# Where ScalarE's function tables are loaded in the first block's attention stage

## What is computed

```python
z = h @ w_in
q, k, v = heads(z[..., :ATT_W]), heads(...), heads(...)
att = _neighbourhood_attention(q, k, v, kc, vc, rpb, rows)   # softmax over a window and a context

def _spatial_gating(u, v, ln_g, ln_b, w_s, b_s):
    u = jax.nn.gelu(u)
    v = _layernorm(jax.nn.gelu(v), ln_g, ln_b)
    ...
    return u * mixed

def _conformer_conv(a, gate, w, b, ng, nb):
    h = a * jax.nn.sigmoid(gate)
    ...
    return jax.nn.silu(h)
```

## Time and profile before

| | us |
|---|---|
| median of 3 runs | 1346.89 |
| lowest and highest | 1346.85, 1347.02 |
| the profiled execution | 1347.08 |
| its span, first to last instruction | 1345.8 |
| PE busy in the span | 1328.6 |
| ACT busy in the span | 628.7 |
| DVE busy in the span | 826.0 |

### The profile page before, as it was taken

One profiled execution on the slowest core, in us unless ns is written; L12 is line 12 of the kernel. 1 busy time (PEld: TensorE's weight loads), 2 busy tenths in 40 slices (PEclk: granted clock), 3 DMA queues, 4 the chain that ended last, 5 costly groups with the idle time before them and its releaser, 6 DMA issues.

```text
span 1345.8 us, 17461 instructions
## 1 busy us (share of the span) xinstructions
PE 1328.6 (99%) x6892; PEld 1105.1 (82%) x6892; DVE 826.0 (61%) x1171; ACT 628.7 (47%) x911; POOL 54.7 (4%) x73
## 2 busy tenths in 40 slices
PE   9999999999999999999999999999999999999998
PEld 6787877888888888889887787788898888888886
DVE  5679876685554443335535544444877865667897
ACT  6646768453333333223434455333734333434764
POOL 0000000000001111111000000000000500000000
PEclk9999999999999999999999999999999999999999
DMA  9734412323367677776232111223604625323764
GB/s 378 309 123 149 147 54 81 135 95 141 141 189 192 175 191 180 200 184 168 85 111 77 63 64 71 71 94 111 202 17 164 266 94 141 110 95 117 223 208 133
DMA packets 55152, 193.46 MB, mean 144 GB/s; under 512 B 6368, under 2 KB 8672, under 8 KB 53664
## 3 DMA queue, kind: packets, MB, share of 16 engines
q1 hardware_dynamic: 46448, 156.04, 34.1%
q0 software_dynamic: 8624, 36.31, 10.9%
HBM read 184.46 MB, written 28.05 MB: 158 GB/s over the span
## 4 chain that ended last, share of the span: by engine, by line
PE 91%; DVE 5%; ACT 2%; issue 1%; DMA 0%; SPq 0%; DVEq 0%; ACTq 0%
PE banks L681 25%; PE banks L685 24%; PE banks L682 24%; PE banks L1437 3%; PE banks L1438 3%; PE banks L1436 3%; PE banks L1002 1%; PE banks L845 1%; PE banks L985 1%; PE banks L856 1%; PE banks L848 1%; DVE w_lo L2079 1%; PE banks L1293 1%; PE banks L1257 1%; PE banks L818 1%
## 5 line engine op out<-in xcount | busy, mean ns | idle before, releaser
L681 PE MATMUL banks<-h_hi,w_hi 128*128 128x512 f32 (+1 forms) x1248 | 470.0, 378 | 2.5 <-DVE w_lo L2079 2.0
L682 PE MATMUL banks<-h_hi,w_lo 128*128 128x512 f32 (+1 forms) x1248 | 465.4, 375 | 0.0
L685 PE MATMUL banks<-h_lo,w_hi 128*128 128x512 f32 (+1 forms) x1248 | 460.6, 375 | 0.8 <-DVE h_lo L2433 0.2
L2079 DVE TENSOR_TENSOR w_lo<-raw_w,w_hi 128x1024 fp32r<-128x1024 f32 (+2 forms) x215 | 252.5, 1180 | 239.0 <-ACT w_hi L1474 238.8
L1474 ACT ACTIVATE w_hi<-raw_w 128x1024 fp32r<-128x1024 f32 (+2 forms) x215 | 214.5, 1003 | 191.7 <-PE banks L685 169.5
L681 PEld LDWEIGHTS banks<-h_hi,w_hi 128*128 128x128 f32 x1248 | 234.9, 188 | 49.8 <-issue 6.0
L685 PEld LDWEIGHTS banks<-h_lo,w_hi 128*128 128x128 f32 x1248 | 231.4, 188 | 44.7 <-DVE h_lo L2433 1.7
L682 PEld LDWEIGHTS banks<-h_hi,w_lo 128*128 128x128 f32 x1248 | 235.1, 188 | 40.3
L681 PE MATMUL banks<-a_hi,w_hi 128*128 128x512 f32 (+1 forms) x198 | 72.5, 366 | 0.0
L682 PE MATMUL banks<-a_hi,w_lo 128*128 128x512 f32 (+1 forms) x198 | 72.4, 366 | 0.0
L685 PE MATMUL banks<-a_lo,w_hi 128*128 128x512 f32 (+1 forms) x198 | 72.4, 366 | 0.0
(11 more groups left out here) (353 smaller groups left out, 1911.6 us busy)
## 6 DMA issues: line engine op xcount, KB each, us to landing
raw_w<-in_w_ffn_up SPq DMA_DIRECT2D x44, 512.0 KB, 4.3
raw_w<-in_w_up SPq DMA_DIRECT2D x44, 512.0 KB, 4.1
down_sums<-in_w_down POOLq DMA_DIRECT2D x40, 512.0 KB, 5.3
raw_w<-down_sums SPq DMA_DIRECT2D x25, 512.0 KB, 4.0
raw_w<-in_ada_rows SPq DMA_DIRECT2D x24, 512.0 KB, 4.1
early<-in_ada_turned SPq DMA_DIRECT2D x8, 1024.0 KB, 18.1
raw_w<-in_w_gates SPq DMA_DIRECT2D x16, 512.0 KB, 3.2
raw_w<-in_w_ffn_down SPq DMA_DIRECT2D x16, 448.0 KB, 4.0
```

Of the source, the lines that this page charges most:

```text
L681: e.matmul(dst, lhs_hi, rhs_hi, start=first, stop=False)
L682: e.matmul(dst, lhs_lo, rhs_hi, start=False, stop=False)
L685: return e.matmul(dst, lhs_hi, rhs_lo, start=False, stop=last)
L2079: e.tensor_tensor(lo[:, 0:n], raw[:, i % RAW, 0:n], hi[:, 0:n].bitcast(F32), ALU.subtract).then_inc(s_lo, 1)
```

## The change

Line numbers behind the edits differ by up to 14. In `after_product` a load of Exp's table is asked for right behind the curve of `g1`, `v0`, `v1`, `u0` and `u1`, ahead of `prepare`. In the walk over `MIXER`, behind `copy_over(i)` for i up to 10, the table of a curve is asked for if a group with a curve ends before the next `turn`. No other engine's program changes.

```diff
--- before.py
+++ after.py
@@ -1624,11 +1624,15 @@
                     out = grid_of(bank[b][:, :])
                     if group[0] == "g":
                         e.activation(rows_of(cv_in[:, c, PAD:PAD + T]), out, ACT.Sigmoid).then_inc(s_cv_gate, 1)
+                        if c:
+                            e.preload_act_table(ACT.Exp)
                     elif group[0] == "v":
                         e.activation(rows_of(sg_vT[:, c, :]), out, ACT.Gelu_apprx_tanh).then_inc(s_gelu_v, 1)
+                        e.preload_act_table(ACT.Exp)
                     elif group[0] == "u":
                         e.wait_ge(s_sg_turned, 2)
                         e.activation(rows_of(sg_out[:, c, :]), out, ACT.Gelu_apprx_tanh).then_inc(s_gelu_u, 1)
+                        e.preload_act_table(ACT.Exp)
                 if group != "a1":
                     prepare(t + 4)
 
@@ -1655,6 +1659,14 @@
                 else:
                     e.wait_ge(s_sg_done, n - 1)
                     split_hi(sg_out[:, n - 2, :], h_hi[:, OUT_ORDER[n], :], s_mix_hi)
+
+            turns = [at for at, step in enumerate(MIXER) if step[0] == "turn"]
+            curves = {"g": ACT.Sigmoid, "v": ACT.Gelu_apprx_tanh, "u": ACT.Gelu_apprx_tanh}
+
+            def curve_after_turn(i):
+                for step in MIXER[turns[i]:turns[i + 1]]:
+                    if step[0] == "product" and step[-1] and step[1][0] in curves:
+                        return curves[step[1][0]]
 
             for kind, *of in MIXER:
                 if kind == "scores":
@@ -1676,6 +1688,8 @@
                         mixed_hi(2)
                         mixed_hi(3)
                     copy_over(of[0])
+                    if of[0] < LAST_HEADS - 1 and curve_after_turn(of[0]):
+                        e.preload_act_table(curve_after_turn(of[0]))
                     if of[0] == LAST_HEADS - 1:
                         normalised(LAST_HEADS)
                 elif kind == "values":
```

## The result

| | median us | lowest to highest | executions |
|---|---|---|---|
| before | 1346.98 | 1346.81 to 1348.77 | 20 |
| after | 1348.90 | 1348.44 to 1350.78 | 20 |

The ratio is 1.0016, with a 95% interval from 1.001 to 1.0022: the change costs 1.9 us, between 1.3 and 3.0 us. The forecast was 1348.5, in a range from 1347.2 to 1349.7. It expected a difference too small to be told from none; with 20 executions of each kernel it can just be told, at 0.16%.

What follows compares the result with a forecast made beforehand. TensorE bounds the kernel, busy 1328.6 of 1345.8 us, so ScalarE edits count only through PE's waits. Costs 1.42 + 0 + 0.22 = 1.64 us on the median 1346.89 gave 1348.5 us, range 1347.2 to 1349.7.

Steps and rivals of the forecast that it cites:

- Part 1: After g1: Exp's load ahead of w_hi delays the chain to turn 0, costing PE 1.42 us.
- Part 2: At v0 and v1: early curve tables and Exp's load ahead of w_hi neither cost nor gain anything.
- cover of 2.1 us: At turn 4: scaled probabilities end near 139.0, PE wants them at 141.16; without this room, 1.14 us lost.
- Part 3: At u0: gelu's table, thrown out by the square root's, is one load too many; scores 9 wait 1.29 us.
- the 0.04 that I had put on the root: At u0's gating norm: the root ends at 168.75 instead of DVE's 168.71, so PE's wait grows by 0.04 us.
- Part 4: At u1: the old 1.01 us wait of scores 10 absorbs most of the 1.29 us, leaving 0.22 us.
- near-tie: At scores 10: PE ready at 184.48, ACT's exponents 9 allowing the start at 184.50.
- The slower rival: At scores 10: exponents 9 come late, the give-back fails, run takes 1349.6 to 1350.6 us; chance 6 in 100.
- a load that holds ACT for twice its row: At moved loads: ACT stands still another 1.38 us, after g1 2.80 us, run 1349.9 us; chance 1 in 100.

Runs made afterwards that it cites:

- changed_again: The kernel after, unchanged, run once more beside the kernel with matmuls filling the wait; median 1348.88 us, ratio 1.0017.
- only_g1: The kernel before with only Exp's table load behind g1's curve, ahead of the weight tile; median 1348.51 us, ratio 1.0013.
- load_behind_tile: The kernel after without the gelu load behind copy 6, and with g1's Exp load moved behind the weight tile's preparation; median 1346.00 us, ratio 0.9992.
- only_v: The kernel before with the edits of v0 and v1 alone; median 1347.10 us, ratio 1.0.
- two_g1_loads: The kernel after with a second table load, gelu's, ahead of the Exp load behind g1; median 1351.33 us, ratio 1.0029.

## Why the prediction was right, and what it missed

The profile of changed_again has no fall of the clock, so its steps can be set against the prediction's. PE of changed_again; all times below are counted from `turn` 0, which starts at 102.97 here and at 101.74 before, so that the two profiles are compared apart from part 1:

```profile
102.97 1.24 PE L985 MATMUL banks<-consts_sb,squares 128*128 128x128 f32 x8 [1.73 <-ACT squares L1596]
...
173.91 1.09 PE L1026 MATMUL banks<-sg_small_sb,sg_v 128*64 128x128 f32 x16 [0.57 <-DVE sg_v L2315]
...
177.05 0.70 PE L973 MATMUL banks<-k_loc,q_loc 64*128 64x256 f32 x4 [1.17 <-ACT squares L1589]
...
185.71 0.70 PE L973 MATMUL banks<-k_loc,q_loc 64*128 64x256 f32 x4
```

**Part 1, 1.42 us.** The wait of `turn` 0 is 1.73 in place of 0.30, that is 1.43 more. The walk through `w_hi`, `w_lo`, modulation row, tap and reciprocal held. only_g1 has the cost alone (1.40), and load_behind_tile shows that it is the place and not the load.

**Part 2, nothing.** ACT of changed_again around `v0` (before in the earlier trace rows):

```profile
126.37 1.28 ACT L1692 ACT_TABLE_LOAD   x1
128.85 1.33 ACT L1596 ACTIVATE normed<-normed,soft 128x512 f32<-128x512 f32 x2 [1.20 <-DVE soft L2291]
131.21 0.60 ACT L1630 ACTIVATE sg_out<-banks 128x512 f32<-128x512 f32 x1 [1.02 <-PE banks L685]
131.83 1.28 ACT L1631 ACT_TABLE_LOAD   x1
133.12 1.06 ACT L1474 ACTIVATE w_hi<-raw_w 128x1024 fp32r<-128x1024 f32 x1
```

The early table shortens ACT's idle time ahead of the scaling from 2.50 to 1.20 us, and then the curve waits 1.02 us for v0's product: the table was not what held it. `w_hi` starts at 133.12 less 102.97 = 30.15, and at 130.75 less 101.74 = 29.01 before: 1.14 later, for 1.13 forecast. The cover of 2.1 us ahead of `turn` 4 was enough, and only_v shows no difference. `v1` is not quite of the same shape: its curve follows the scaling at once in changed_again (scaling from 138.93, curve from 140.17), so there the product does not hold it; it makes no difference to PE either.

**Part 3, a new wait at `scores` 9.** ACT of changed_again around `u0` (before in the earlier trace rows):

```profile
164.73 1.28 ACT L1692 ACT_TABLE_LOAD   x1
166.02 0.42 ACT L1650 ACTIVATE sg_square<-sg_v 128x256 f32<-128x256 f32 x1
...
168.35 1.28 ACT L1652 ACT_TABLE_LOAD   x1
...
171.19 1.28 ACT L1634 ACT_TABLE_LOAD   x1
```

Gelu's table at 164.73 is thrown out by the root's at 168.35 and loaded again at 171.19. `scores` 9 start 74.08 us after `turn` 0, and 72.79 before: 1.29 later, the forecast's number. The wait itself is 1.17, in the forecast's 1.1 to 1.3. The gating product at L1026 starts 70.94 after `turn` 0 instead of 70.90, the 0.04 that I had put on the root. One detail I did not see: its wait is shorter than before, 0.57 for 0.71, since the scaling behind the root is late as well and makes `turn` 7 ahead of it take longer; the root ends the stretch either way, so the time is the same.

**Part 4, the give-back.** `scores` 10 start 82.74 after `turn` 0, and 82.54 before: 0.20 later, for 0.22 forecast, and without a wait. The two candidates of the near-tie, PE at 184.48 and ACT at 184.50, came out with PE last. The slower rival, that exponents 9 come too late for the give-back, did not happen; had it, the wait of 1.0 us at `scores` 10 would have stayed.

**The sum.** 1.43 + 0.20 is 1.63 us. The 13 executions of after that are not long have their median at 1348.55, 1.57 above before's. So the walk holds to within 0.1 us.

**What it missed.** The step that was incomplete is the first: a wait of PE was costed at its own length. In about a third of the executions with a wait of 1.7 us at `turn` 0 the clock falls, most likely because of it, and the long executions of after stand some 1.2 to 2.2 us above the median of the others. That lifts the median from 1348.55 to 1348.90, and the mean by more. It is small here since most executions escape it; the range still held the median, though not each execution. That the median stayed inside is in part luck: had more than half of the executions been long, as in two_g1_loads, it would have stood at 1349.71 or above. Of the rivals, a load that holds ACT for twice its row is ruled out: the second load of two_g1_loads adds 1.28 us, and where nothing else holds the next ACTIVATE, it starts 0.01 to 0.02 us behind the load (96.66 + 1.28 against 97.96). The Trainium skill (ScalarE: Activation LUTs, What ACT_TABLE_LOAD costs) gives some 1380 ns of drain on top of 1283 ns; the trace agrees with the second and shows none of the first, and here the measurement decides.

## What to carry to other kernels

Where the busiest engine seldom waits, a preload on another engine is worth just the wait that it removes there, and its price is read from what is queued right behind it: Exp's load behind `g1` cost 1.4 us ahead of a weight tile and nothing behind it, and gelu's load, moved into idle time, gained 1.1 us at the only curve that PE's next wait hung on. Before a table is loaded early, look for any other function between the load and its use, which throws it out. A new wait is not lost for good if PE waits again soon after; but a new wait of TensorE, of 1.7 us here, can cost more than its length, since the clock may fall behind it: look at the granted clock and at many executions, not at one profile.

## What the runs showed of the hardware

TensorE's granted clock fell to half behind one wait of 1.73 us in a run that keeps it busy 99% of the time, and the fall cost 1.7 us, about as much as the wait. It began about 1.6 us after the wait had ended (1.1 us in two_g1_loads), amid matmuls, so its cost stands in the profile as busy time and not as a wait. It came in 15 of 42 executions with a wait of 1.7 us, in 8 of 11 with 3.0 us, and in 2 of 22 where matmuls filled the wait (counted by the length of the executions; seen in the profiled ones of after and two_g1_loads, and absent behind the wait of 1.73 and 1.72 us in those of changed_again and only_g1). Waits for a transfer of up to 2.34 us near the start of the run show no fall behind them in any profile. The Trainium skill (TensorE: Matmul & The Clock Gate, HAM oscillation — how this bites in real kernels) tells of a kernel whose clock falls at its waits for data in every tile; here a single wait was followed by a fall, and only in some of the executions of one program.
